# Two transformer blocks on one core: 0/1-matrix products given rounded part and remainder, and halves of squares added by VectorE

## The chip, the cores and the metric

The program runs on one NeuronCore of a Trainium2 chip. The time is device microseconds (us) of one execution of the whole program; lower is better.

## The reference, cut to what matters

`reference(...)` runs two blocks over 256 tokens of 1024 features. The first block mixes tokens with a spatial gate and a bidirectional gated linear attention (four heads, value width 256), whose outputs are normed per head: `o = o * rsqrt(mean(o*o) + eps)`. A convolutional feed-forward follows. The second block prepends 16 tokens (272 in all), runs a gated DeltaNet layer with eight heads of width 128 in chunks, and then feed-forwards and a short-convolution mixer. In the DeltaNet layer three parts matter here:

```
a_mat = I + strict_lower((k_beta @ k.T) * decay)      # one per chunk and head
u = triangular_solve(a_mat, v_beta, lower=True)
...
o = o * rsqrt(mean(o * o, axis=-1) + RMS_EPS) * norm_w   # per token and head
```

## The kernel before, in words

Features lie on the 128 partitions, tokens along the free dimension. Every linear layer is cut in units of eight 128x128 weight blocks. A weight unit `w_raw` is loaded by SyncE, rounded to float32r by ScalarE (`w_hi`, helper line L1689), its remainder `w_lo` is formed by GpSimd (L673), and TensorE multiplies three single-pass float32r products, hi-hi, hi-lo and lo-hi (L763, L785, L788, L948). Small products that need full precision run as plain float32; each of these appears in the trace as two matmul passes with a weight load each. The order of work on each engine is written out by hand. PSUM banks are passed on through counting semaphores: `banks_free` for the weight tiles in banks 0 to 3, and `taken[b]` with the table `TURN` for stages of the second block. `stage_done` counts finished TensorE stages.

**First block, output squares.** ScalarE squares the attention outputs into `osq` (four heads, two halves, 256 tokens). `output_squares` (L1243 to L1251) multiplies each half by a matrix of constants 1/256, two products per head that accumulate, between the linear layers `w_ga` and `w_gb`. ScalarE then takes the root into `orstd` (L1959 to L1963) and only after that counts `banks_free`, for which the first tile of `w_gb` waits. VectorE's part of this stretch is at L2893 to L2903: gate the outputs, form eight remainders of `gu`, add halves of the `w_ga` tiles.

**Second block, 16-row solves.** The blocks of 16 on the diagonals of the triangular matrices are gathered in `diag16` (24 matrices of 16 columns: 16 from bank 4 through a ScalarE copy at L2257, 8 of the short first chunk written by VectorE in `key_products`, L3196). `spread_rows` (L1384 to L1396) copies row k of each block to all 16 partitions of that block, for k = 0 to 14, by a product with the 0/1 matrix `pick16[:, k]` of 128x128; row k has 24 x (15-k) columns, 360 down to 24. These 15 float32 products are spread over six bank turns `sp0` to `sp5`. ScalarE copies each bank to `spread` and VectorE eliminates (`eliminate`, L3211 to L3218, two chained operations for each k). In VectorE's order this stands between the convolution taps (`taps(11, 12, 13)` at L3388). In TensorE's order `blocks_by_lane`, tile 13 of `a_in`, `spread_rows` and tiles 14 to 17 follow each other. The inverses are then flipped by TensorE (`fI1`, `fI2`), copied by ScalarE and VectorE, and their banks 4 to 7 are taken over by the products `kq1` and `kq2` (L1343).

**Second block, norm factors.** `factor` (L3481 to L3490) sums head squares on VectorE and takes a reciprocal. `norm_root` (L2354 to L2359) takes a root on ScalarE into row 5 of `tok`. `factors` (L1522 to L1529) spreads the eight rows over 128 partitions by float32 products with the 0/1 matrix `sel`, with 8 rows as contraction: 8 heads of 134 tokens (`nbA`, `nbB`, `nbC`) and 8 heads of 128 tokens (`nb2A`, `nb2B`). VectorE and ScalarE gate, round and form remainders (L3513 to L3521), and the layer `a_out` (L948) waits for these head by head.

```
ins = mm(dst, pick16[:, k], diag16[:, :, k + 1:], start=True, stop=True)
ins = mm(banks[BANKS[name][0]][:, i * n:(i + 1) * n], sel[:, hh], tok[:, 5, t0_:t1_], start=True, stop=True)
```

Of the kernel before, what the change touches and what calls it, by code (L numbers as in the profile page):

```python
# [17 lines left out]
F32 = mybir.dt.float32  # L18
# [71 lines left out]
def bass_two_blocks(nc, a, out):  # L90
    ctx = ExitStack()
    with ctx:
# [3 lines left out]
        def at(name, shape, offset, dt=F32):  # L96
            return nc.alloc_sbuf_tensor_at(name, shape, dt, offset=offset)
# [164 lines left out]
        pick16 = at("pick16", [P, BLOCK - 1, P], area_a + 17536)  # L262
        spread = [at(f"spread{i}", [P, 512], area_x + 2048 * i if i < 4 else area_a + 25216 + 2048 * (i - 4)) for i in range(6)]
        diag16 = at("diag16", [P, 3 * HN, BLOCK], arena + 41984)
# [438 lines left out]
        def _(pe):  # L703
# [538 lines left out]
            def output_squares():  # L1242

                for b in range(2):
                    pe.wait_ge(banks_free, TILE0["oms"] + b + 1)
                    pe.wait_ge(osq_ready, 4)
                    for hh in (2 * b, 2 * b + 1):
                        for half in range(2):
                            ins = mm(banks[b][:, (hh % 2) * N1:(hh % 2 + 1) * N1], over_dv, osq[:, hh, half],
                                     start=(half == 0), stop=(half == 1))  # L1250
                    ins.then_inc(oms_done, 1)  # L1251

            by_blocks("w_vs", 2, 0)
# [130 lines left out]
            def spread_rows():  # L1384


                pe.wait_ge(spread_ready, 2)
                read_out("kk0")
                read_out("cd")
                for name, ks in SPREAD.items():  # L1390
                    claim(name)
                    for k in ks:
                        o_, n = SPREAD_AT[k][1], BLOCK - 1 - k
                        dst = banks[BANKS[name][0]][:, o_:o_ + 3 * HN * n].rearrange("p (a n) -> p a n", n=n)
                        ins = mm(dst, pick16[:, k], diag16[:, :, k + 1:], start=True, stop=True)
                    ins.then_inc(stage_done, 1)  # L1396

            def y(c, lv):
# [124 lines left out]
            def factors(name, heads, t0_, t1_):  # L1523

                claim(name)
                n = t1_ - t0_
                for i, hh in enumerate(heads):
                    ins = mm(banks[BANKS[name][0]][:, i * n:(i + 1) * n], sel[:, hh], tok[:, 5, t0_:t1_], start=True, stop=True)
                ins.then_inc(stage_done, 1)  # L1529

            def ba(k):
# [147 lines left out]
        def _(act):  # L1679
# [8 lines left out]
            def fn(out_, in_, f, **kw):  # L1688
                return nc.scalar.activation(out_, in_, f, **kw)  # L1689
# [560 lines left out]
            squared(10)  # L2250
            product_out(2, 3)
            tap3(12)
            rounded(12)
            activated(11)
            squared(11)
            act.wait_ge(stage_done, DONE["cd"])
            fn(diag16[:, 0:2 * HN], banks[4][:, 0:2 * P].rearrange("p (a i) -> p a i", i=BLOCK), ACT.Copy).then_inc(taken[4], 1)  # L2257
            tap3(13)
            rounded(13)
            activated(12)  # L2260
# [93 lines left out]
            def norm_root(j, bank, tk):  # L2354

                act.wait_ge(inv_ms, j + 1)
                fn(tok[:, 5, tk], banks[bank][0:HN, 0:tk.stop - tk.start], ACT.Sqrt).then_inc(taken[bank], 1)
                act.wait_ge(taken[bank], TURN[("ho01", "ho2")[j], bank] + 1)
                act.sem_inc(factor_ready, 1)  # L2359

            a_norm = column("a_norm", 0)

# [263 lines left out]
        def _(dve):  # L2626
# [561 lines left out]
            def key_products(c, exp):  # L3188

                cn, B = CHUNKS[c][1], cb[c]  # L3190
                dve.wait_ge(dd_exp, exp)
                for heads, src, free in staged(f"kk{c}", cn, cn):
                    n = src.shape[1]
                    for i in range(n):
                        hh = heads.start + i
                        dst = src[:, i] if c else diag16[0:cn, 2 * HN + hh]  # L3196
                        ins = v.scalar_tensor_tensor(dst, src[:, i], per_token(c, 5, hh), B["dd"][0:cn, hh],
                                                     ALU.mult, ALU.mult)
                    if c == 0:
                        ins.then_inc(free, 1)  # L3200
                        continue
                    ins.then_inc(mt_scaled, 1)

            def identities():

                v.memset(diag16[:, 2 * HN:], 0.0).then_inc(spread_ready, 1)
                dve.wait_ge(taken[7], TURN["inv", 7])
                link(v.tensor_copy(inv16, lanes(eye16[:], 3 * HN)))

            def eliminate(k0, k1_):  # L3210

                for k in range(k0, k1_):
                    n, (name, o_) = BLOCK - 1 - k, SPREAD_AT[k]
                    b = BANKS[name][0]
                    dve.wait_ge(taken[b], TURN[name, b] + 1)
                    row = spread[list(SPREAD).index(name)][:, o_:o_ + 3 * HN * n].rearrange("p (a n) -> p a n", n=n)
# [265 lines left out]
            def factor(j, name, tk):  # L3482

                dve.wait_ge(stage_done, DONE[name])
                total, n = tok[:, 9, tk], tk.stop - tk.start
                for g in range(4):
                    part = banks[BANKS[name][0]][32 * g:32 * g + HN, 0:n]
                    link(v.scalar_tensor_tensor(total, part, 1 / P, total, ALU.mult, ALU.add))
                bank = banks[BANKS[name][0]][0:HN, 0:n]
                v.reciprocal(bank, total).then_inc(inv_ms, 1)  # L3490

            outputs("ov1", 0, 1, 2)
            outputs("ov1", 1, 1, 3)
# [548 lines left out]
```

## Time and profile before

| | |
|---|---|
| three runs | 1243.83, 1244.70, 1246.42 us |
| median | 1244.7 us |
| span of the profiled execution | 1243.2 us |
| TensorE busy, matmuls | 1223.5 us (98%) |
| VectorE, ScalarE, GpSimd busy | 736.0, 722.2, 880.3 us |
| mean granted TensorE clock | 0.993 |

The time of the profiled execution is listed only as its span, from the first to the last instruction; what lies around it isn't listed apart. PE is TensorE's matmuls, PEld its weight loads, DVE VectorE, ACT ScalarE, POOL GpSimd. A row of a timeline gives the start, the duration, the engine, the line and the number of merged instructions; idle time ahead of a row stands in square brackets with what ended it. TensorE's matmuls are pipelined, so the time that each takes from the stream is the distance between starts and not its duration.

### The profile page before, as it was taken

Reading aid. Unit: us, or ns where it says so; the run is one execution under the profiler, and the core shown is the slowest. Engines: PE = TensorE matmul, PEld = TensorE weight load, DVE = VectorE, ACT = ScalarE, POOL = GpSimd, SP = SyncE. Lnnn points to the kernel's source line nnn. Section 1 sums busy time; section 2 is a strip of 40 time slices with the busy share of each in tenths; the row PEclk is TensorE's granted clock in tenths of the full one; section 3 lists DMA queues with packets and bytes.
Section 4 is the critical chain, followed back from the end, with each engine's and each line's share of the span. In section 5 each row is a group of like instructions: output and inputs, shape, how many; then the busy total and the mean of one; then the engine's idle time right before and its main releaser. Section 6 shows DMA issues by size and latency. Waiting matters only on the chain.

```text
span 1243.2 us, 26081 instructions
## 1 busy us (share of the span) xinstructions
PE 1223.5 (98%) x9026; PEld 1127.9 (91%) x9026; DVE 736.0 (59%) x1718; ACT 722.2 (58%) x1325; POOL 880.3 (71%) x387
## 2 busy tenths in 40 slices
PE   9999999999999999999999999999999999999997
PEld 3678899988998888889999999999999999999986
DVE  3989972244587774159884375555634757555633
ACT  3656654565666665479642366666655547666753
POOL 0357857568869888957533248888898868888795
PEclk9999999999999999999998999999999999999999
DMA  9995355446646665645332126555566555656562
GB/s 369 408 366 186 102 187 153 119 149 205 183 142 210 190 186 164 188 146 162 118 98 75 52 88 190 182 183 172 159 187 196 174 166 170 193 180 185 154 200 71
DMA packets 66038, 217.76 MB, mean 175 GB/s; under 512 B 9904, under 2 KB 17328, under 8 KB 62624
## 3 DMA queue, kind: packets, MB, share of 16 engines
q1 hardware_dynamic: 65952, 216.59, 55.0%
q8 instruction: 57, 0.93, 0.3%
q14 instruction: 29, 0.24, 0.1%
HBM read 215.52 MB, written 1.05 MB: 174 GB/s over the span
## 4 chain that ended last, share of the span: by engine, by line
issue 38%; POOL 37%; PE 22%; ACT 1%; POOLq 1%; DVE 1%; ACTq 0%; DVEq 0%
POOL w_lo L673 36%; PE bank L802 10%; PE bank L1135 5%; PE bank L894 3%; PE bank L903 1%; PE bank L898 1%; POOL w_lo L680 1%; POOLq L670 0%; ACT h L1689 0%; ACT w_hi L1689 0%; POOLq L672 0%; PE bank L948 0%; PE bank L724 0%; PE bank L729 0%; PE bank L725 0%
## 5 line engine op out<-in xcount | busy, mean ns | idle before, releaser
L673 POOL TENSOR_TENSOR w_lo<-w_raw,w_hi 128x1024 fp32r<-128x1024 f32 x340 | 812.8, 2404 | 325.1 <-ACT w_hi L1689 323.7
L1689 ACT ACTIVATE w_hi<-w_raw 128x1024 fp32r<-128x1024 f32 (+1 forms) x372 | 378.1, 1020 | 103.0 <-PE bank L903 34.8
L802 PE MATMUL bank<-a_hi,w_hi 128*128 128x264 f32 (+3 forms) x704 | 200.5, 285 | 0.6 <-DVE a_lo L3670 0.6
L802 PE MATMUL bank<-a_hi,w_lo 128*128 128x264 f32 (+3 forms) x704 | 200.2, 284 | 0.0
L802 PE MATMUL bank<-a_lo,w_hi 128*128 128x264 f32 (+3 forms) x704 | 199.9, 284 | 0.0
L802 PEld LDWEIGHTS bank<-a_hi,w_hi 128*128 128x128 f32 x704 | 132.9, 189 | 0.8 <-DVE a_lo L3670 0.8
L802 PEld LDWEIGHTS bank<-a_lo,w_hi 128*128 128x128 f32 x704 | 132.9, 189 | 0.1
L802 PEld LDWEIGHTS bank<-a_hi,w_lo 128*128 128x128 f32 x704 | 132.9, 189 | 0.0
L3745 DVE SCALAR_TENSOR_TENSOR bank<-row_mean,cols,bank 128x260 f32<-128x260 f32 (+3 forms) x112 | 54.6, 488 | 115.8 <-ACT cols L1689 113.0
L763 PE MATMUL bank<-a_parts,w_hi 128*128 128x256 f32 x448 | 81.5, 284 | 0.5 <-DVE a_parts L2952 0.4
L894 PE MATMUL bank<-g_parts,w_hi 128*128 128x512 f32 x308 | 78.9, 396 | 0.0
L680 POOL TENSOR_TENSOR w_lo<-w_raw,w_hi x32 | 58.1, 1844 | 24.0 <-ACT w_hi L1689 23.1
L3042 DVE SCALAR_TENSOR_TENSOR cbuf<-bank,pv,cbuf 128x189 f32<-128x189 f32 (+2 forms) x176 | 65.7, 424 | 14.4 <-ACT cbuf L1689 13.8
L763 PE MATMUL bank<-a_hi,w_hi 128*128 128x272 f32 (+1 forms) x240 | 72.2, 301 | 0.4 <-POOL w_lo L673 0.4
L763 PEld LDWEIGHTS bank<-a_parts,w_hi 128*128 128x128 f32 x448 | 69.8, 192 | 1.2 <-DVE a_parts L2952 0.6
L763 PE MATMUL bank<-a_hi,w_lo 128*128 128x272 f32 (+1 forms) x240 | 70.3, 293 | 0.0
L763 PE MATMUL bank<-a_lo,w_hi 128*128 128x272 f32 (+1 forms) x240 | 70.2, 293 | 0.0
L785 PE MATMUL bank<-a_parts,w_hi 128*128 128x512 f32 x256 | 64.3, 393 | 0.3 <-ACTq L1963 0.3
L894 PEld LDWEIGHTS bank<-g_parts,w_hi 128*128 128x128 f32 x308 | 54.9, 188 | 10.2
L808 PE MATMUL bank<-a_parts,w_hi 128*128 128x512 f32 x256 | 64.1, 392 | 0.0
L931 PE MATMUL bank<-g_parts,w_hi 128*128 128x260 f32 x352 | 63.8, 284 | 0.0
L763 PE MATMUL bank<-a_parts,w_lo 128*128 128x256 f32 x224 | 63.4, 283 | 0.0
(548 smaller groups left out, 2933.1 us busy)
## 6 DMA issues: line engine op xcount, KB each, us to landing
w_raw<-in_s SPq DMA_DIRECT2D x284, 512.0 KB, 3.6
w_raw<-in_down SPq DMA_DIRECT2D x48, 512.0 KB, 3.5
adaw<-in_w_ada SPq DMA_DIRECT2D x16, 1024.0 KB, 9.7
w_raw<-in_down SPq DMA_DIRECT2D x24, 384.0 KB, 3.3
adab<-in_w_ada_first SPq DMA_DIRECT2D x8, 1024.0 KB, 8.7
ctxt<-in_ctx SPq DMA_DIRECT2D x1, 1024.0 KB, 11.3
x<-in_x SPq DMA_DIRECT2D x1, 1024.0 KB, 15.3
out_h<-h SPq DMA_DIRECT2D x4, 256.0 KB, 2.6
```

What stands on the lines that cost most here:

```text
L673: pool.tensor_tensor(w_lo[:, s], w_raw[:, s], w_hi[:, s].bitcast(F32), ALU.subtract) \
L680: pool.tensor_tensor(w_lo[:, :, ds(k, 1)], w_raw[:, :, ds(k, 1)], w_hi[:, :, ds(k, 1)].bitcast(F32), ALU.subtract) \
L763: ins = mm(banks[s][:, first:n], w_[:, s, k], x_[:, k, first:n], start=(m == 0), stop=(m == 3 * KD - 1))
L785: mm(banks[s][:, :].rearrange("p (two n) -> p two n", two=2), w_hi[:, s, k], a_parts[:, :, k, cols], start=(k == 0), stop=False)
L802: ins = mm(banks[bank][:, tk], w_[:, s, k], x_[:, k, tk], start=(m == 0), stop=(m == 3 * KD - 1))
L808: mm(banks[bank][:, :].rearrange("p (two n) -> p two n", two=2), w_hi[:, s, k], a_parts[:, :, k, N1:], start=(k == 0), stop=False)
L894: mm(dst[:, :].rearrange("p (two n) -> p two n", two=2), w_hi[:, s, k], g_parts[:, :, kk, first:n], start=(kk == 0), stop=False)
L931: ins = mm(banks[t][:, first:N2], w_[:, s, k], x_[:, k0 + k, first:N2], start=(m == 0), stop=(m == 3 * KF - 1))
L1135: ins = mm(banks[b][:, :].rearrange("p (u m) -> p u m", u=SLOTS), x_[:, k, tk], w_[:, :, k], start=(k == 0 and i == 0), stop=(k == KD - 1 ...
L1689: return nc.scalar.activation(out_, in_, f, **kw)
L3042: v.scalar_tensor_tensor(dst, frm(banks[banks_of(p)[0]][:, 0:n]), pv[:, ds(pair + w, 1)], dst, ALU.mult, ALU.add).then_inc(conv_seq, 1)
L3745: return v.scalar_tensor_tensor(dst, row_mean[:, N2 - dst.shape[-1]:], by, dst, ALU.mult, ALU.add)
```

## The change

Three edits. `pick16` becomes float32r; the diagonal blocks are stored row-major (`[P, 16, 24]`) as a rounded part `diag_hi` and a remainder `diag_lo`, each row is spread by two accumulating float32r products, and the spread rows lie column-major. The head factors are stored as rounded part in rows 0 to 7 and remainder in rows 32 to 39 of `rows_r`, and each head is spread by one float32r product with contraction 128. The two halves of each head's output squares are added by VectorE, so that one product per head is left.

```diff
-                pe.wait_ge(osq_ready, 4)
+                pe.wait_ge(osq_ready, 5)
 for hh in (2 * b, 2 * b + 1):
-    for half in range(2):
-        ins = mm(banks[b][...], over_dv, osq[:, hh, half], start=(half == 0), stop=(half == 1))
+    ins = mm(banks[b][...], over_dv, osq[:, hh, 0], start=True, stop=True)
 ...
 # VectorE, after the four o_gated products, ahead of the gu remainders
+v.tensor_tensor(osq[:, :, 0], osq[:, :, 0], osq[:, :, 1], ALU.add).then_inc(osq_ready, 1)
 ...
 # spread_rows, TensorE
-pe.wait_ge(spread_ready, 2)
+pe.wait_ge(spread_ready, 3)
-dst = banks[...][:, o_:o_ + 3 * HN * n].rearrange("p (a n) -> p a n", n=n)
-ins = mm(dst, pick16[:, k], diag16[:, :, k + 1:], start=True, stop=True)
+dst = banks[...][:, o_:o_ + 3 * HN * n].rearrange("p (n a) -> p n a", n=n)
+mm(dst, pick16[:, k], diag_hi[:, k + 1:], start=True, stop=False)
+ins = mm(dst, pick16[:, k], diag_lo[:, k + 1:], start=False, stop=True)
 ...
 # ScalarE: ahead of rounded(12) instead of behind squared(11)
+act.wait_ge(stage_done, DONE["cd"])
+fn(diag_hi[:, :, 0:2 * HN].rearrange("p i a -> p a i"), banks[4][:, 0:2 * P]..., ACT.Copy).then_inc(taken[4], 1)
 rounded(12)
 activated(11)
 squared(11)
-act.wait_ge(stage_done, DONE["cd"])
-fn(diag16[:, 0:2 * HN], banks[4][:, 0:2 * P]..., ACT.Copy).then_inc(taken[4], 1)
 ...
 # VectorE
-taps(11, 12, 13)
+dve.wait_ge(taken[5], TURN["kk0", 5] + 1)
+link(v.tensor_copy(diag_hi[:, :, 2 * HN:], diag16[:].rearrange("p a i -> p i a")))
+v.tensor_tensor(diag_lo[:, :, 2 * HN:], diag16[:]..., diag_hi[:, :, 2 * HN:]..., ALU.subtract).then_inc(spread_ready, 1)
+taps(11, 12)
+dve.wait_ge(taken[4], TURN["cd", 4] + 1)
+v.tensor_tensor(diag_lo[:, :, 0:2 * HN], banks[4][:, 0:2 * P]..., diag_hi[:, :, 0:2 * HN]..., ALU.subtract).then_inc(spread_ready, 1)
+taps(13)
 ...
 # eliminate: the spread row is read with a step of 24 elements
-row = spread[...][:, o_:o_ + 3 * HN * n].rearrange("p (a n) -> p a n", n=n)
+row = spread[...][:, o_:o_ + 3 * HN * n].rearrange("p (n a) -> p a n", n=n)
 ...
 # factors, TensorE
-ins = mm(banks[...][:, i * n:(i + 1) * n], sel[:, hh], tok[:, 5, t0_:t1_], start=True, stop=True)
+ins = mm(banks[...][:, i * n:(i + 1) * n], sel_r[:, hh], rows_r[:, 0, t0_:t1_], start=True, stop=True)
 ...
 # norm_root, ScalarE
-fn(tok[:, 5, tk], banks[bank][...], ACT.Sqrt).then_inc(taken[bank], 1)
-act.wait_ge(taken[bank], TURN[("ho01", "ho2")[j], bank] + 1)
-act.sem_inc(factor_ready, 1)
+fn(tok[:, 5, tk], src, ACT.Sqrt)
+fn(rows_r[0:HN, 0, tk], src, ACT.Sqrt).then_inc(taken[bank], 1)
 ...
 # factor, VectorE, behind the reciprocal
+dve.wait_ge(taken[b], TURN[name, b] + 1)
+v.tensor_tensor(rows_r[32:32 + HN, 0, tk], tok[:, 5, tk], rows_r[0:HN, 0, tk]..., ALU.subtract).then_inc(factor_ready, 1)
```

## Rows read from the trace of the kernel before

**Rows 1.** The profile's page: span, and TensorE's busy time.

```profile
span 1243.2 us, 26081 instructions
PE 1223.5 (98%) x9026; PEld 1127.9 (91%) x9026; DVE 736.0 (59%) x1718; ACT 722.2 (58%) x1325; POOL 880.3 (71%) x387
```

**Rows 2.** Busy by stretch: length, PE, PEld, DVE, ACT, POOL, granted clock, DMA, GB/s.

```profile
667.00:674.00 7.00, 7.00 (x52) 6.61 (x51) 2.24 (x5) 0.75 (x2) 1.26 (x1) 0.51 0.26 77
...
721.00:726.00 5.00, 5.00 (x31) 5.00 (x30) 4.37 (x10) 3.17 (x6) 2.02 (x1) 0.66 0.36 102
```

**Rows 3.** Timeline, all engines, around the output squares of the first block.

```profile
251.99 3.62 PE L1249 MATMUL bank<-osq,averages 128*128 128x256 f32 x16
...
253.42 0.38 ACT L1689 ACTIVATE ga<-bank 128x256 f32 x1
...
253.81 1.28 ACT L1689 ACT_TABLE_LOAD   x1
255.10 1.49 ACT L1689 ACTIVATE orstd<-bank,eps 128x512 f32<-128x512 f32 x2
...
255.89 2.12 PE L785 MATMUL bank<-a_parts,w_hi 128*128 128x512 f32 x8 [0.28 <-ACTq L1963]
```

**Rows 4.** Timeline, TensorE, the spread rows and the tile behind them.

```profile
597.47 5.77 PE L1395 MATMUL bank<-diag,pick 128*128 128x360 f32 x30
603.08 0.37 PE L763 MATMUL bank<-a_hi,w_hi 128*128 128x272 f32 x1
```

**Rows 5.** Timeline, TensorE, eight float32r products of 512 and eight of 256 columns.

```profile
249.19 2.00 PE L785 MATMUL bank<-a_parts,w_hi 128*128 128x512 f32 x8
251.04 1.11 PE L788 MATMUL bank<-a_parts,w_lo 128*128 128x256 f32 x8
```

**Rows 6.** Timeline, VectorE, from the taps to the elimination.

```profile
594.47 3.02 DVE L3154 SCALAR_TENSOR_TENSOR qr<-bank,pv,qr 128x269 f32<-128x269 f32 x6
598.01 1.57 DVE L3154 SCALAR_TENSOR_TENSOR qr<-bank,pv,qr 128x269 f32<-128x269 f32 x3 [0.53 <-ACT qr L1689]
600.21 0.53 DVE L3217 TENSOR_TENSOR term<-spread,bank 128x360 f32<-128x360 f32 x1 [0.64 <-ACT spread L1689]
...
610.84 0.28 DVE L3217 TENSOR_TENSOR term<-spread,bank 128x120 f32<-128x120 f32 x1
```

**Rows 7.** Timeline, ScalarE, copies of the first three bank turns.

```profile
599.61 1.53 ACT L1689 ACTIVATE spread<-bank 128x504 f32<-128x504 f32 x3
```

**Rows 8.** Timelines, the flipped inverses: VectorE's copies, and the products behind them.

```profile
621.09 1.28 DVE L3259 COPY tt<-bank 128x512 f32<-128x512 f32 x2
...
621.71 3.84 PE L1343 MATMUL bank<-qr,kr 128*128 128x128 f32 x32 [0.26 <-ACT tt L1689]
```

**Rows 9.** Timelines, TensorE, VectorE and ScalarE around the norm factors.

```profile
708.37 1.60 PE L1528 MATMUL bank<-tok,sel_r 8*128 8x134 f32 x12 [0.78 <-ACT mt L1689]
...
709.90 0.49 PE L1519 MATMUL bank<-qr,s2b 128*128 128x128 f32 x2
...
717.17 0.95 DVE L3490 RECIPROCAL bank<-tok 8x128 f32<-8x128 f32 x1
...
718.15 0.27 ACT L1689 ACTIVATE tok<-bank 8x128 f32<-8x128 f32 x1 [3.29 <-DVE bank L3490]
...
718.58 2.05 PE L1528 MATMUL bank<-tok,sel_r 8*128 8x128 f32 x16
```

**Rows 10.** Timelines, VectorE's last remainders and the eighth block of `a_out`.

```profile
726.48 0.62 DVE L3521 SCALAR_TENSOR_TENSOR a_lo<-bank,pv,a_hi 128x134 fp32r<-128x134 f32 x2 [0.24 <-ACT a_hi L1689]
...
727.68 0.28 PE L948 MATMUL bank<-a_hi,w_hi 128*128 128x262 f32 x1
```

**Rows 11.** Instructions of three VectorE lines: durations in ns, start in us.

```profile
L2670 DVE TENSOR_REDUCE eye<-ident x1: 368/368/368, 3.6 to 3.6; 128x16 f32<-128x128 f32 x1
...
L2675 DVE TENSOR_REDUCE block_of<-ident x1: 275/275/275, 4.2 to 4.2; 128x8 f32<-128x128 f32 x1
...
L3350 DVE TENSOR_TENSOR rows_r<-tok,rows_r x1: 1930/1930/1930, 563.0 to 563.0; 8x272 fp32r<-8x272 f32 x1
```

More of the change, by code:

```diff
@@ L260, in bass_two_blocks @@
         cb[2]["vb"] = at("vb2", [P, HN, P], area_a + 17536 + 8704)
-        pick16 = at("pick16", [P, BLOCK - 1, P], area_a + 17536)
+        pick16 = at("pick16", [P, BLOCK - 1, P], area_a + 17536, F32R)
         spread = [at(f"spread{i}", [P, 512], area_x + 2048 * i if i < 4 else area_a + 25216 + 2048 * (i - 4)) for i in range(6)]
-        diag16 = at("diag16", [P, 3 * HN, BLOCK], arena + 41984)
+        diag16 = at("diag16", [P, HN, BLOCK], arena + 41984)
+        diag_hi = at("diag_hi", [P, BLOCK, 3 * HN], arena + 54272, F32R)
+        diag_lo = at("diag_lo", [P, BLOCK, 3 * HN], arena + 55808, F32R)
         term16 = at("term16", [P, 3 * HN, BLOCK - 1], arena + 43520)
@@ L1245, in output_squares @@
                     pe.wait_ge(banks_free, TILE0["oms"] + b + 1)
-                    pe.wait_ge(osq_ready, 4)
+                    pe.wait_ge(osq_ready, 5)
                     for hh in (2 * b, 2 * b + 1):
-                        for half in range(2):
-                            ins = mm(banks[b][:, (hh % 2) * N1:(hh % 2 + 1) * N1], over_dv, osq[:, hh, half],
-                                     start=(half == 0), stop=(half == 1))
+                        ins = mm(banks[b][:, (hh % 2) * N1:(hh % 2 + 1) * N1], over_dv, osq[:, hh, 0], start=True, stop=True)
                     ins.then_inc(oms_done, 1)
@@ L1393, in spread_rows @@
                         o_, n = SPREAD_AT[k][1], BLOCK - 1 - k
-                        dst = banks[BANKS[name][0]][:, o_:o_ + 3 * HN * n].rearrange("p (a n) -> p a n", n=n)
-                        ins = mm(dst, pick16[:, k], diag16[:, :, k + 1:], start=True, stop=True)
+                        dst = banks[BANKS[name][0]][:, o_:o_ + 3 * HN * n].rearrange("p (n a) -> p n a", n=n)
+                        mm(dst, pick16[:, k], diag_hi[:, k + 1:], start=True, stop=False)
+                        ins = mm(dst, pick16[:, k], diag_lo[:, k + 1:], start=False, stop=True)
                     ins.then_inc(stage_done, 1)
@@ L1527, in factors @@
                 for i, hh in enumerate(heads):
-                    ins = mm(banks[BANKS[name][0]][:, i * n:(i + 1) * n], sel[:, hh], tok[:, 5, t0_:t1_], start=True, stop=True)
+                    ins = mm(banks[BANKS[name][0]][:, i * n:(i + 1) * n], sel_r[:, hh], rows_r[:, 0, t0_:t1_], start=True, stop=True)
                 ins.then_inc(stage_done, 1)
@@ L2252, in _ @@
             tap3(12)
+            act.wait_ge(stage_done, DONE["cd"])
+            fn(diag_hi[:, :, 0:2 * HN].rearrange("p i a -> p a i"), banks[4][:, 0:2 * P].rearrange("p (a i) -> p a i", i=BLOCK), ACT.Copy).then_inc(taken[4], 1)
             rounded(12)
@@ L2255, in _ @@
             squared(11)
-            act.wait_ge(stage_done, DONE["cd"])
-            fn(diag16[:, 0:2 * HN], banks[4][:, 0:2 * P].rearrange("p (a i) -> p a i", i=BLOCK), ACT.Copy).then_inc(taken[4], 1)
             tap3(13)
@@ L2356, in norm_root @@
                 act.wait_ge(inv_ms, j + 1)
-                fn(tok[:, 5, tk], banks[bank][0:HN, 0:tk.stop - tk.start], ACT.Sqrt).then_inc(taken[bank], 1)
-                act.wait_ge(taken[bank], TURN[("ho01", "ho2")[j], bank] + 1)
-                act.sem_inc(factor_ready, 1)
+                src = banks[bank][0:HN, 0:tk.stop - tk.start]
+                fn(tok[:, 5, tk], src, ACT.Sqrt)
+                fn(rows_r[0:HN, 0, tk], src, ACT.Sqrt).then_inc(taken[bank], 1)
             a_norm = column("a_norm", 0)
@@ L3195, in key_products @@
                         hh = heads.start + i
-                        dst = src[:, i] if c else diag16[0:cn, 2 * HN + hh]
+                        dst = src[:, i] if c else diag16[0:cn, hh]
                         ins = v.scalar_tensor_tensor(dst, src[:, i], per_token(c, 5, hh), B["dd"][0:cn, hh],
@@ L3204, in identities @@
             def identities():
-                v.memset(diag16[:, 2 * HN:], 0.0).then_inc(spread_ready, 1)
+                v.memset(diag16[:], 0.0)
                 dve.wait_ge(taken[7], TURN["inv", 7])
@@ L3215, in eliminate @@
                     dve.wait_ge(taken[b], TURN[name, b] + 1)
-                    row = spread[list(SPREAD).index(name)][:, o_:o_ + 3 * HN * n].rearrange("p (a n) -> p a n", n=n)
+                    row = spread[list(SPREAD).index(name)][:, o_:o_ + 3 * HN * n].rearrange("p (n a) -> p a n", n=n)
                     link(v.tensor_tensor(term16[:, :, 0:n], row, inv16[:, :, k:k + 1].broadcast_to([P, 3 * HN, n]), ALU.mult))
@@ L3387, in _ @@
             key_products(0, 3)
-            taps(11, 12, 13)
+            dve.wait_ge(taken[5], TURN["kk0", 5] + 1)
+            link(v.tensor_copy(diag_hi[:, :, 2 * HN:], diag16[:].rearrange("p a i -> p i a")))
+            v.tensor_tensor(diag_lo[:, :, 2 * HN:], diag16[:].rearrange("p a i -> p i a"), diag_hi[:, :, 2 * HN:].bitcast(F32), ALU.subtract).then_inc(spread_ready, 1)
+            taps(11, 12)
+            dve.wait_ge(taken[4], TURN["cd", 4] + 1)
+            v.tensor_tensor(diag_lo[:, :, 0:2 * HN], banks[4][:, 0:2 * P].rearrange("p (a i) -> p i a", i=BLOCK),
+                            diag_hi[:, :, 0:2 * HN].bitcast(F32), ALU.subtract).then_inc(spread_ready, 1)
+            taps(13)
             eliminate(0, 7)
@@ L3490, in factor @@
                 v.reciprocal(bank, total).then_inc(inv_ms, 1)
+                b = BANKS[name][0]
+                dve.wait_ge(taken[b], TURN[name, b] + 1)
+                v.tensor_tensor(rows_r[32:32 + HN, 0, tk], tok[:, 5, tk], rows_r[0:HN, 0, tk].bitcast(F32), ALU.subtract) \
+                    .then_inc(factor_ready, 1)
             outputs("ov1", 0, 1, 2)
```

## The prediction

> **What bounds the kernel now.** I read the page first. TensorE is busy for 98% of a span of 1243.2 us [rows 1], so its stream sets the time, and an edit counts only by what it takes out of that stream or what idle time it puts in. Then I read the clock by stretches. It is at full speed (2.4 GHz) almost everywhere. It falls to half, 1.2 GHz, for about 7 us from 667 on, after a run of small 64-row products, and for about 3.4 us from 721.9 on, after the norm factors [rows 2]. At last I read the three places of the change in the timelines: what TensorE does, and which other engine it meets next. The sums are against the profiled execution, whose own time is listed only as the span; 1243.2 is 1.5 us under the median of 1244.7, and I carry the differences over to the median.
>
> **Output squares.** Now 8 products are 16 passes of 256 columns. Their starts are (3.62 - 0.38) / 15 = 0.216 us apart [rows 3], that is 0.84 ns a column. The edit takes out 8 passes, 1.7 us of TensorE. But who waits next? The first tile of `w_gb` waits for ScalarE's root of the first bank. ScalarE ends the last sigmoid of `w_ga` at 253.80, loads the table for the root for 1.28 us and begins the root at 255.10. TensorE has ended its squares just before and still waits 0.28 us, until 255.89 [rows 3]. None of ScalarE's steps follows from the squares: with two products the first bank is full at 253.0 instead of 253.9, both before 255.10. So TensorE stops 1.7 us earlier and restarts at the same 255.89: the wait grows from 0.3 to 2.0 us and the gain is nothing. VectorE's new add has 1024 columns. By VectorE's slope, (0.53 - 0.28) us over 240 columns [rows 6], it takes some 1.2 us. Behind it stand the eight `gu` remainders and the first half-sum of `w_ga`, for which ScalarE's sigmoid waits; the bank of that tile is wanted only four tiles (11 us) later, so I cost the delay at nothing. **Term: 0.0.**
>
> **Spread rows.** Now the 15 products, 30 passes, run from 597.47 to 603.08, 5.61 us [rows 4]. At 0.84 ns for each of 2 x 2880 columns that is 4.9 us. Take off 0.3 us of a bank wait; what is left, 0.4 us, falls on the narrow passes, which therefore stand at least about 0.10 us apart, against 0.02 us of columns in the narrowest. I read that as the weight load of 128 columns.
>
> After the change there are 30 float32r products of the same widths. Eight products of 512 columns stand (2.00 - 0.39) / 7 = 0.230 us apart, of 256 columns (1.11 - 0.28) / 7 = 0.118 [rows 5]: 0.44 ns a column and 0.006 us. No row shows a float32r product under 256 columns, and ten of the fifteen widths are under it. The cheapest that I can argue is the weight-load floor, 0.105 us; the dearest is what float32 pays for the same columns in its two passes, 1.69 ns each. I take the cheap end, since the rows from 512 to 256 columns lie on one line. Then the widths 360 to 240 give 0.164 + 0.153 + 0.143 + 0.132 + 0.122 + 0.111 and nine others 0.105 each: 1.77 us, twice 3.5 us.
>
> The start moves too. VectorE began `taps(11)` at 594.47 and now first does a copy and a subtraction of 128 elements, 0.3 us each by the 120-element row, and a link: 0.6 us. Taps 11 and 12 take 3.0 us, then comes the new subtraction of 256 elements, about 0.43 us between the rows of 120 and 360 [rows 6]. It ends at 594.47 + 0.6 + 3.0 + 0.43 = 598.5, so TensorE starts at 598.6 instead of 597.47: a new stall of 1.1 us. Behind it ScalarE's copies still begin at 599.61, as ScalarE is busy with tile 13 until then, and end 0.5 us apart [rows 7]. The fourth turn waits for the first copy (600.2), the fifth for the second (600.65), the sixth for the third (601.2); the sixth has ten products, 1.05 us. End 602.25 against 603.08: 0.8 us gained of 2.1. The ScalarE copy that moves ahead of a weight rounding delays that rounding by 1 us; its unit is wanted four tiles, over 9 us, later: nothing.
>
> Does the 0.8 survive? VectorE begins the elimination at 600.21 as before and is busy without a break until its copies of the flipped inverses, from 621.09 to 622.3. TensorE starts the products behind them at 621.71 and needs VectorE's first copy (done 621.73) only for the second four heads, 0.9 us on [rows 8]. So it can come up to 0.9 us earlier. **Term: -0.8.**
>
> **Norm factors.** The first 12 passes take 709.90 - 708.37 = 1.53 us [rows 9]; six float32r products at 0.12 us take 0.7: -0.8. Their start is set by a bank and hides the second root and the new subtraction. Further on the second group's chain has no slack: the reciprocal ends at 718.12, the root at 718.42, and the products start at 718.58 [rows 9]. A second root (0.2) and a subtraction with its hop (0.35) come in, partly against a slack of 0.1: +0.45 for these products. They shrink from 1.98 us to about 0.95. TensorE thus gains about 1.4 us until `a_in`'s last tile. Then `a_out` wants remainders head by head. VectorE's last ends at 727.10, TensorE needs it at 727.68 [rows 10]; that chain moves by -0.8 + 0.2 (the second root ahead of ScalarE's rounding) = -0.6, to 726.5. TensorE arrives no later than 726.4 even if the clock falls again, so VectorE's chain ends last: 727.68 - 726.5. **Term: -1.2.**
>
> **Sum:** 0.0 - 0.8 - 1.2 = -2.0 us: span 1241.2, median 1242.7.
>
> **A rule against the change.** The elimination's 15 multiplications read 2880 elements of spread rows one after another; each element now lies 96 bytes from the last. Two early reductions over the same 128 elements show what a step may cost: 368 ns with 64 bytes between elements, 275 ns in order [rows 11], 0.73 ns an element. For 2880 that would be 2.1 us; if the 93 ns are the cost of shorter groups it is nothing, which I take as likelier. The Trainium skill, SBUF — State Buffer, on cachelines, says that each access that crosses to another 16-byte line pays a penalty. By that rule the multiplications are slower, and the two reductions agree with it in sign. A second row matters for the new subtractions whose inputs both lie in SBUF: L3350 took 1.93 us for 272 columns [rows 11], where 0.43 would be expected. If the one at 595 meets the same, TensorE's stall grows by up to 1.5 us; that end I keep for the range. The same page, on the shared port pair, says that a VectorE instruction with two SBUF inputs is blocked for the length of a GpSimd instruction that reads SBUF.
>
> **Rivals.**
> - *Narrow float32r products at float32's price.* For: no product under 256 columns is in the trace. Against: nothing but the line from 512 to 256. Ten widths at 1.69 ns a column (floor 0.105) give 2.3 us, five wide ones 0.7, twice 3.0 = 6.1 us from 598.6 on: TensorE goes on at 604.7, +1.6. The factors gain 0.2 before and lose 0.35 in the chain: +0.2. Time 1246.5, slower than before; it decides from a price of about 1.2 ns a column on, where the stall is no longer paid back.
> - *Stepped reads cost 0.73 ns an element.* VectorE's chain grows 2.1 us, of which 0.9 is slack at the flipped inverses: +1.2 instead of -0.8. Time 1244.7.
> - *The squares do gain*, if ScalarE's table load follows them after all: -1.7 more, 1241.0. The load begins right at the end of the sigmoid [rows 3], which speaks against it.
> - *The clock.* Idle or thinner work may bring one more stretch at half clock, or take one away: 3.4 us at half cost 1.7 us [rows 2], 1244.4 or 1241.0 from the forecast.
>
> **How the numbers follow.** Forecast 0.42; narrow price 0.30; stepped reads 0.18; squares 0.03; clock or other 0.07. The range: 1240.9 to 1247.0 takes in a clock stretch less on one side, the narrow price and part of a blocked subtraction on the other. A measurement here tells some 0.2%, 2.5 us, from no change. My forecast of -2.0 lies just inside; with the scatter of runs (1243.8 to 1246.4) I give it a 0.4 chance to pass: 0.17, and 0.08 from the squares and the clock. The narrow price passes +2.5 in a third: 0.10, others 0.05. Faster 0.25, same 0.60, slower 0.15.
>
> **What would show it.** The squares: L785's idle ahead of `w_gb` at 2.0 us, orstd's start against the sigmoid's end unchanged. The spread: TensorE's idle ahead of it 1.1 us, and the distance of starts of the 96-column products, 0.105 or 0.16. The elimination: L3217 at 360 columns 0.53 or 0.8 us. The factors: starts 0.12 us apart, or 0.22. The prediction is wrong if `w_gb` starts earlier after the sigmoid, if the narrow starts are at the float32 price, or if TensorE waits for VectorE at the flipped inverses.

## The result and the profile after

The changed kernel takes 1247.88 us (median of 10 runs, 1245.13 to 1250.29) against 1244.8 us before (10 runs, 1243.83 to 1246.42): ratio 1.0023, interval 1.0015 to 1.0032. That is slower by 2.9 us, where 2.0 us faster was forecast, and outside the range of 1240.9 to 1247.0. The profiled execution took 1248.83 us, span 1247.0. From the profile's page of the changed kernel:

```profile
span 1247.0 us, 26039 instructions
PE 1222.0 (98%) x9002; PEld 1126.4 (90%) x9002; DVE 741.0 (59%) x1724; ACT 722.8 (58%) x1327; POOL 881.4 (71%) x387
```

VectorE is busy for 741.0 us instead of 736.0; TensorE's share of 98% is the old one [rows 1]. Next the table of TensorE's waits in the changed kernel, dearest first (what it waited for, us in total, times, longest):

```profile
PE bank L1316 <- ACT ksq L1690: 2.6, 1, 2.6
PE bank L787 <- ACTq L1964: 2.0, 1, 2.0
...
PE bank L1395 <- DVE diag_lo L3395: 1.1, 1, 1.1
...
PE bank L950 <- DVE a_lo L3534: 0.9, 2, 0.6
```

The waits ahead of `w_gb` (L787) and of the spread products (L1395) were forecast, at 2.0 and 1.1 us. The first, 2.6 us for ScalarE's `ksq`, stands nowhere in the prediction. Two places in TensorE's timeline of the changed kernel, the squares [rows 3] and the spread rows [rows 4]:

```profile
251.62 1.89 PE L1250 MATMUL bank<-osq,averages 128*128 128x256 f32 x8
255.52 3.29 PE L787 MATMUL bank<-a_parts,w_hi 128*128 128x512 f32 x8 [2.01 <-ACTq L1964]
...
599.11 0.43 PE L1395 MATMUL bank<-diag_hi,pick 128*128 128x360 f32 x1 [1.14 <-DVE diag_lo L3395]
...
602.05 0.26 PE L1395 MATMUL bank<-diag_hi,pick 128*128 128x96 f32 x1
602.15 0.28 PE L1396 MATMUL bank<-diag_lo,pick 128*128 128x96 f32 x1
...
602.92 0.37 PE L765 MATMUL bank<-a_hi,w_hi 128*128 128x272 f32 x1
```

From squares to `w_gb` are 3.90 us, as before. The narrow float32r products start 0.10 us apart: the cheap price, so the rival with 0.30 of the chance is out at once. From the end of the tile ahead (599.11 - 1.14 = 597.97) to the next tile are 4.95 us, where before there were 603.08 - 597.47 = 5.61: 0.66 gained, 0.8 forecast. The stage itself does what was said. Now VectorE's timeline behind it [rows 6], and TensorE's at the next meeting, the key norms and the products behind the flipped inverses [rows 8]:

```profile
595.39 0.38 DVE L3392 TENSOR_TENSOR diag_lo<-diag,diag_hi 128x128 fp32r<-128x128 f32 x1
...
598.64 0.41 DVE L3395 TENSOR_TENSOR diag_lo<-bank,diag_hi 128x256 fp32r<-128x256 f32 x1
598.97 1.56 DVE L3156 SCALAR_TENSOR_TENSOR qr<-bank,pv,qr 128x269 f32<-128x269 f32 x3
600.79 0.95 DVE L3219 TENSOR_TENSOR term<-spread,bank 128x360 f32<-128x360 f32 x1 [0.27 <-ACT spread L1690]
601.78 0.54 DVE L3220 TENSOR_TENSOR bank<-bank,term 128x360 f32<-128x360 f32 x1
...
615.20 1.57 DVE L3156 SCALAR_TENSOR_TENSOR qr<-bank,pv,qr 128x269 f32<-128x269 f32 x3
```

```profile
617.75 1.86 PE L1316 MATMUL bank<-ksq,pick 128*8 128x272 f32 x16 [2.57 <-ACT ksq L1690]
...
625.64 3.84 PE L1343 MATMUL bank<-qr,kr 128*128 128x128 f32 x32 [0.27 <-ACT tt L1690]
```

The multiplication of 360 columns takes 0.95 us instead of 0.53; the sum behind it, whose operands are all in PSUM or in order, still 0.54. The fifteen multiplications take 8.52 us together, where before they took 5.34: 3.2 us more, and the elimination also begins 0.58 later. Inside the elimination stands the last tile of taps of `qr` (615.20 here, 611.48 before). ScalarE squares it, and TensorE's key norms wait for that square. Before, the square was there at 614.3, 1.1 us ahead of TensorE at 615.38; now it is 2.6 us late.

Last, the granted clock. Stretches of the changed kernel (start and end in us, length, TensorE busy, granted clock, DMA share, GB/s):

```profile
255.00:260.00 5.00, 4.48 (x17) 0.66 0.53 175
617.00:622.00 5.00, 4.25 (x29) 0.66 0.35 105
641.00:646.00 5.00, 4.76 (x66) 0.66 0.38 111
672.00:680.00 8.00, 8.00 (x64) 0.57 0.23 68
```

Half clock falls in this execution behind the idle 2.0 us ahead of `w_gb`, behind the idle 2.6 us ahead of the key norms, and behind the small 32-row products at 641; the stretch at 672 was there before, and the one behind the norm factors [rows 2] is gone. Counted together that is two stretches of 3.4 us more than before, some 1.7 us each.

### The profile page after: what moved, and what is told of

It is laid out like the page before. It is cut to its first block, busy times and chain, and to the rows that moved or that the text cites. A ratio compares the mean times of both kernels' runs of the same rounds, so it can differ in the third digit from the quotient of the medians.

```text
span 1247.0 us, 26039 instructions
## 1 busy us (share of the span) xinstructions
PE 1222.0 (98%) x9002; PEld 1126.4 (90%) x9002; DVE 741.0 (59%) x1724; ACT 722.8 (58%) x1327; POOL 881.4 (71%) x387
## 4 chain that ended last, share of the span: by engine, by line
issue 38%; POOL 37%; PE 22%; ACT 1%; POOLq 1%; DVE 1%; ACTq 0%; DVEq 0%
POOL w_lo L675 37%; PE bank L804 10%; PE bank L1137 5%; PE bank L896 3%; PE bank L905 1%; PE bank L900 1%; POOL w_lo L682 1%; POOLq L672 0%; ACT h L1690 0%; ACT w_hi L1690 0%; POOLq L674 0%; PE bank L726 0%; PE bank L950 0%; PE bank L731 0%; PE bank L727 0%
## 5 line engine op out<-in xcount | busy, mean ns | idle before, releaser
L787 PE MATMUL bank<-a_parts,w_hi 128*128 128x512 f32 x256 | 65.5, 398 | 2.0 <-ACTq L1964 2.0
```

The lines of the kernel that those rows point to most:

```text
L787: mm(banks[s][:, :].rearrange("p (two n) -> p two n", two=2), w_hi[:, s, k], a_parts[:, :, k, cols], start=(k == 0), stop=False)
```

## The experiments

All comparisons are with the kernel before, run on the same chip beside them: 1244.54 us (31 runs) for the first four, 1244.4 us (33 runs) for the next four, 1244.3 us (17 runs) for the last three.

### The three edits one at a time, and the order alone

**e_sq** is the kernel before with only this:

```diff
-                    pe.wait_ge(osq_ready, 4)
+                    pe.wait_ge(osq_ready, 5)
-                        for half in range(2):
-                            ins = mm(..., osq[:, hh, half], start=(half == 0), stop=(half == 1))
+                        ins = mm(..., over_dv, osq[:, hh, 0], start=True, stop=True)
+            v.tensor_tensor(osq[:, :, 0], osq[:, :, 0], osq[:, :, 1], ALU.add).then_inc(osq_ready, 1)
```

> Before with the squares' edit alone. Theory A (the idle time costs clock): TensorE stops 1.7 us earlier, w_gb still starts where it did, idle ahead of it 2.0 us instead of 0.3, and the clock falls to half for some 3.4 us right behind it, which costs 1.7 us: 1246.4 us. Theory B (the edit is neutral, the half-clock stretch seen there belongs to something else): 2.0 us of idle, clock full, 1244.7 us.

Measured: 1245.29 us, ratio 1.0006 (0.9997 to 1.0015). Timeline of TensorE and the clock of two stretches in its profiled execution:

```profile
251.99 1.89 PE L1248 MATMUL bank<-osq,averages 128*128 128x256 f32 x8
255.89 2.12 PE L785 MATMUL bank<-a_parts,w_hi 128*128 128x512 f32 x8 [2.01 <-ACTq L1961]
...
255.00:260.00 5.00, 4.11 (x22) 1.00 0.58 186
637.00:642.00 5.00, 5.00 (x55) 0.66 0.38 108
```

`w_gb` starts at 255.89, to the hundredth where it started before [rows 3]: the idle time took the whole saving. The same 2.0 us of idle time left the clock at full here and at half in the changed kernel; instead half clock came at 638, where the profiled execution of before has none, and the stretch behind the norm factors [rows 2] stayed away, so the two executions spent the same time at half clock. So theory A's 1.7 us are not paid each time. Over the runs the mean granted clock is 0.9937 against 0.9945 before; 0.0008 of 1243 us is 1.0 us, and the means of the spans differ by 0.9 (1243.8 against 1242.9). The ratio's interval holds 1, so a cost of the squares' edit is not shown, only that it brings nothing.

**e_fac** is the kernel before with only this:

```diff
-  ins = mm(banks[...][:, i * n:(i + 1) * n], sel[:, hh], tok[:, 5, t0_:t1_], start=True, stop=True)
+  ins = mm(banks[...][:, i * n:(i + 1) * n], sel_r[:, hh], rows_r[:, 0, t0_:t1_], start=True, stop=True)
+  fn(rows_r[0:HN, 0, tk], src, ACT.Sqrt).then_inc(taken[bank], 1)
+  v.tensor_tensor(rows_r[32:32 + HN, 0, tk], tok[:, 5, tk], rows_r[0:HN, 0, tk]..., ALU.subtract).then_inc(factor_ready, 1)
```

> Before with the factors' edit alone. Theory A: the products start 0.118 us apart or less and TensorE is 1.2 to 1.6 us earlier at a_in's last tile; a_out then waits for VectorE's remainders, about -1.0 us in all, 1243.7 us, and 1242.0 if the half-clock stretch behind the factors goes as it did in the changed kernel. Theory B (the gain in the changed kernel was the clock's alone, the new root and subtraction eat the rest): 1244.7 us.

Measured: 1242.48 us, ratio 0.9981 (0.9971 to 0.999): the edit gains 2.1 us. TensorE's timeline:

```profile
704.75 0.86 PE L1528 MATMUL bank<-rows_r,sel_r 128*128 128x134 f32 x6 [0.78 <-ACT mt L1689]
...
714.43 1.11 PE L1528 MATMUL bank<-rows_r,sel_r 128*128 128x128 f32 x8 [0.29 <-DVE rows_r L3493]
...
721.14 0.39 PE L948 MATMUL bank<-a_hi,w_hi 128*128 128x262 f32 x1 [0.29 <-DVE a_lo L3525]
```

Eight products last 1.11 us, so their starts are (1.11 - 0.28) / 7 = 0.119 apart. Between the first factor product and the eighth block of `a_out` lie 17.65 us here (704.75 to 722.40) and 18.63 in e_sq (709.21 to 727.84), both without half clock in between: 1.0 us is the edit's own. The other 1.1 us of the medians may be the clock's, which these runs do not separate: the mean granted clock rises from 0.9945 to 0.9964, and this execution has no half-clock stretch before 1230 us.

**e_spr** is the kernel before with only the spread edit: the split of the diagonal blocks, fifteen products in two parts, rows laid `(n a)`, and the multiplication reading them with steps.

```diff
+  dst = ...rearrange("p (n a) -> p n a", n=n)
+  mm(dst, pick16[:, k], diag_hi[:, k + 1:], start=True, stop=False)
+  ins = mm(dst, pick16[:, k], diag_lo[:, k + 1:], start=False, stop=True)
-  row = spread[...][:, o_:o_ + 3 * HN * n].rearrange("p (a n) -> p a n", n=n)
+  row = spread[...][:, o_:o_ + 3 * HN * n].rearrange("p (n a) -> p a n", n=n)
```

> Before with the spread edit alone. Theory A (VectorE's stepped reads of the spread rows): L3217's 360-column multiplication takes 0.95 us instead of 0.53, the elimination ends 3.2 to 3.8 us later, TensorE waits about 2.6 us for the squares of tile 15 ahead of the key norms, with a half-clock stretch behind it: 1248 us with one such stretch, 1246.4 with none, 1249.8 with two. Theory B (the cost is the stall of 1.1 us ahead of the products and the two-part products, VectorE's delay being slack): 1244.7 us or below.

Measured: 1247.59 us, ratio 1.0026 (1.0017 to 1.0035). TensorE's timeline at the key norms and behind them:

```profile
619.61 1.10 PE L1318 MATMUL bank<-ksq,pick 128*8 128x272 f32 x16 [2.56 <-ACT ksq L1692]
...
625.28 1.53 PE L1370 MATMUL bank<-ident,uu 128*128 128x128 f32 x12 [0.92 <-DVE tok L3412]
```

The multiplication of 360 columns takes 0.96 us and the wait ahead of the key norms 2.56, as in the changed kernel. The half-clock stretch that theory A put behind this wait did not come: the granted clock from 619 to 624 is 1.00. This profiled execution, the slowest of its eleven runs (1252.43 us), has its half clock at 543, 642, 673 and 717. The three parts alone make +0.06, -0.19 and +0.26 per cent, together +0.13; the whole has +0.23. Each has an interval of about 0.09 to either side, so the parts add up as far as these runs tell.

**e_step** keeps float32 products, without split, subtraction or stall, and changes only the order:

```diff
-  dst = ...rearrange("p (a n) -> p a n", n=n)
+  dst = ...rearrange("p (n a) -> p a n", n=n)
-  row = spread[...]....rearrange("p (a n) -> p a n", n=n)
+  row = spread[...]....rearrange("p (n a) -> p a n", n=n)
```

> Before with the spread rows' order alone: float32 products as before that write each row's 24 groups side by side, and multiplications that read them with 96 bytes between elements; no split, no new subtraction. Theory A (the stepped reads are the cause): multiplications of 360 columns 0.95 us, elimination 3.8 us longer, TensorE waits 2 to 3 us ahead of the key norms, 1247 to 1248.5 us. Theory B (the stepped reads cost little and the two-part form or its stall is the cause): 0.53 to 0.6 us and 1244.7 us.

Measured: 1248.01 us, ratio 1.0023 (1.0013 to 1.0033). The order alone costs as much as the spread edit as a whole. VectorE's and TensorE's timelines:

```profile
599.30 0.95 DVE L3217 TENSOR_TENSOR term<-spread,bank 128x360 f32<-128x360 f32 x1 [0.63 <-ACT spread L1689]
```

```profile
596.61 5.71 PE L1395 MATMUL bank<-diag,pick 128*128 128x360 f32 x30
602.16 0.37 PE L763 MATMUL bank<-a_hi,w_hi 128*128 128x272 f32 x1
...
616.26 1.10 PE L1316 MATMUL bank<-ksq,pick 128*8 128x272 f32 x16 [1.81 <-ACT ksq L1689]
621.93 1.53 PE L1368 MATMUL bank<-ident,uu 128*128 128x128 f32 x12 [0.90 <-DVE tok L3402]
```

The same 0.95 us with no float32r in sight, and TensorE waits twice, 1.8 us for the square of tile 15 and 0.9 for VectorE's row of `tok` behind the copies into blocks. From the first spread product to the products behind the flipped inverses are 26.69 us (596.61 to 623.30) against 24.24 before (597.47 to 621.71), 2.45 more, with the clock full throughout. TensorE's own writes with steps of 96 bytes into PSUM cost it nothing: from the first spread product to the next tile are 5.55 us (596.61 to 602.16), against 5.61 before [rows 4].

### What a step costs

**e_steps** puts twenty multiplications of 360 columns behind the elimination of the kernel before; nothing of it but their durations is used.

```diff
+  for s_ in (1, 2, 3, 4, 6, 8, 12, 24, 60, 120):
+      for src_ in (spread[0], banks[7]):
+          v.tensor_tensor(term as [P, s_, 360 // s_], src_[:, 0:360].rearrange("p (n s) -> p s n", s=s_), one column, ALU.mult)
```

> Before with twenty multiplications of 360 columns put behind the elimination (their results are overwritten unused): ten read one operand from SBUF, ten from PSUM, with 1, 2, 3, 4, 6, 8, 12, 24, 60 and 120 elements between neighbours. Only their durations are wanted. Theory A (a step costs in SBUF, by the line that it crosses to, and not in PSUM): SBUF 0.53 us in order, rising to a plateau of about 0.95 us once neighbours lie 16 bytes or more apart; PSUM 0.53 to 0.58 us at every step. Theory B (the price is one of short runs of elements): SBUF and PSUM alike grow with the number of runs, dearest at 60 and 120.

VectorE's timeline, in the order of the loop. `term<-spread` reads SBUF and `term<-bank` reads PSUM, each pair with the next step. Left out are the second pair (0.53 us both), the SBUF row of 6 elements (0.81) and the PSUM rows of 3 elements (0.54) and of 4, 6, 8, 12 and 60, all 0.53:

```profile
614.50 0.53 DVE L3396 TENSOR_TENSOR term<-spread,bank 128x360 f32<-128x360 f32 x1
615.07 0.53 DVE L3396 TENSOR_TENSOR term<-bank,spread 128x360 f32<-128x360 f32 x1
...
616.76 0.65 DVE L3396 TENSOR_TENSOR term<-spread,bank 128x360 f32<-128x360 f32 x1
...
618.02 0.81 DVE L3396 TENSOR_TENSOR term<-spread,bank 128x360 f32<-128x360 f32 x1
...
620.84 0.80 DVE L3396 TENSOR_TENSOR term<-spread,bank 128x360 f32<-128x360 f32 x1
...
622.25 0.78 DVE L3396 TENSOR_TENSOR term<-spread,bank 128x360 f32<-128x360 f32 x1
...
623.63 0.95 DVE L3396 TENSOR_TENSOR term<-spread,bank 128x360 f32<-128x360 f32 x1
624.62 0.53 DVE L3396 TENSOR_TENSOR term<-bank,spread 128x360 f32<-128x360 f32 x1
625.19 0.81 DVE L3396 TENSOR_TENSOR term<-spread,bank 128x360 f32<-128x360 f32 x1
...
626.60 0.57 DVE L3396 TENSOR_TENSOR term<-spread,bank 128x360 f32<-128x360 f32 x1
627.20 0.53 DVE L3396 TENSOR_TENSOR term<-bank,spread 128x360 f32<-128x360 f32 x1
```

SBUF in order, and with one element between, 0.53; with neighbours 12 bytes apart 0.65; 16 to 48 bytes 0.78 to 0.81; 96 bytes 0.95; 240 bytes 0.81; 480 bytes, where only three elements follow one another, 0.57. PSUM is 0.53 or 0.54 at every step. So SBUF pays for steps and PSUM does not, as theory A says, and theory B, by which both would pay, is out. Theory A's plateau isn't there: 96 bytes is dearer than 16 to 48, and 480 bytes costs almost nothing. Here the run of elements between two jumps back gets shorter as the step grows, so this kernel alone doesn't tell the two apart. Its one execution took 1257.7 us, with the twenty multiplications in it. The Trainium skill, SBUF — State Buffer, on cachelines, puts a penalty on each access that crosses to another 16-byte line. These rows agree for SBUF from 16 bytes on; for the three-element runs, each element on a line of its own, they don't.

### The stepped reads taken away

**e_inv** is the changed kernel with the block inverses and the terms laid out like the spread rows, so that the multiplications read in order. The steps that remain are in PSUM reads.

```diff
-        inv16 = banks[7][...].rearrange("p (a i) -> p a i", i=BLOCK)
+        inv16 = banks[7][...].rearrange("p (i a) -> p a i", i=BLOCK)
-        term16 = at("term16", [P, 3 * HN, BLOCK - 1], arena + 43520)
+        term16 = at("term16", [P, BLOCK - 1, 3 * HN], arena + 43520)
-                    row = ...rearrange("p (n a) -> p a n", n=n)
+                    row = ...rearrange("p (n a) -> p n a", n=n)
+                    inv = inv16.rearrange("p a i -> p i a")
```

> The changed kernel with the elimination's own tiles turned too: the block inverses in PSUM and the terms are laid out with their 24 groups side by side, so that every operand of the multiplications and sums is read in order; the only stepped reads left are those of PSUM by the two copies into blocks. Theory A (the stepped SBUF reads are the cause of the slower time): multiplication of 360 columns 0.53 to 0.58 us, no wait of 2.6 us ahead of the key norms, the copies into blocks 1.17 us each as before, spread edit worth -0.6, with the squares' +0.7 and the factors' -2.0 as measured: 1242.6 us. Theory B (a step costs the same wherever it is read, so the cost moves to the copies into blocks): those copies 1.8 us each or more, 1245 us or above.

Measured: 1243.31 us, ratio 0.9988 (0.9977 to 0.9998), where the changed kernel has 1.0023, each against the kernel before run beside it: 4.6 us between the two medians. VectorE, then TensorE at the key norms:

```profile
601.08 0.53 DVE L3220 TENSOR_TENSOR term<-spread,bank 128x360 f32<-128x360 f32 x1 [0.27 <-ACT spread L1690]
...
616.07 2.33 DVE L3227 TENSOR_TENSOR uu<-bank,block_of 128x1024 f32<-128x1024 f32 x2
```

```profile
615.39 1.10 PE L1316 MATMUL bank<-ksq,pick 128*8 128x272 f32 x16
```

0.53 again, the fifteen multiplications 5.27 us together, no wait ahead of the key norms, and the two copies into blocks, which now read PSUM with steps, take 2.33 us as before. The cost did not move, it is gone. (The squares' 2.0 us of idle time are still in this kernel, and here half clock stands behind them again, 0.66 from 255 to 260.)

### The squares' saving brought into the open

**e_evac** is the kernel before with the squares' edit, and VectorE empties the two banks, so that `w_gb` no longer waits for ScalarE's table load and root. ScalarE's part of the edit isn't shown: it takes the root from VectorE's copy and no longer counts the banks as free.

```diff
+  for b in range(2):
+      dve.wait_ge(oms_done, b + 1)
+      v.tensor_copy(orstd[:, 2 * b:2 * b + 2], banks[b]...).then_inc(ostd_ready, 1)
+  dve.wait_ge(ostd_ready, 2)
+  dve.wait_ge(banks_free, TILE0["oms"] + 4)
+  dve.sem_inc(banks_free, 4)
   for b in range(2):
       ins = v.reciprocal(orstd[:, hs], orstd[:, hs])
+      add_gate_half("w_gb", b)
```

> Before with the squares' edit, and VectorE copies the two banks of mean squares to SBUF and frees them, so that ScalarE's table load and root are no longer between the squares and w_gb; the reciprocal's two halves are followed each by a half-sum of w_gb. Theory A (the 1.7 us of products saved are real, only the root's place hid them): w_gb starts 3.9 - 1.7 = 2.2 us after the squares start, idle about 0.3 us, nothing new behind it: 1244.5 - 1.6 = 1242.9 us. Theory B (VectorE's reciprocal of 6.6 us, which still follows the root, holds the banks and the roundings of w_gb): TensorE waits 1 us or more inside w_gb, 1244 to 1244.7 us.

Measured: 1244.14 us, ratio 0.9997 (0.9988 to 1.0006). The timelines of TensorE and VectorE:

```profile
254.76 2.11 PE L785 MATMUL bank<-a_parts,w_hi 128*128 128x512 f32 x8 [0.87 <-DVEq L2909]
```

```profile
253.93 0.69 DVE L2906 COPY orstd<-bank 128x512 f32<-128x512 f32 x1 [0.17 <-PE bank L1248]
```

`w_gb` starts 2.76 us after the squares instead of 3.90: 1.1 us are there in the trace, and TensorE does not wait inside `w_gb`, so theory B's mechanism is out. The remaining 0.9 us of idle time is the second copy, behind which both banks were freed. The median is where theory B had it all the same, 1.2 us above theory A's: 1.1 us is too small to be told from nothing here.

**e_nospr** is e_evac with the factors' edit, spread rows as before. **e_best** is the changed kernel with e_inv's and e_evac's edits.

> Before with the squares' edit and its early copies, and the factors' edit; spread rows as before. Theory A (the parts add up): -1.6 and -2.0: 1240.9 us. Theory B (the gains are shares of one slack, or of the clock): 1242.5 us.

> The changed kernel with the turned elimination and the early copies of the mean squares: all three edits with what hid or spoiled them taken away. Theory A: -1.6 squares, -0.6 spread rows, -2.0 factors: 1240.3 us. Theory B (the spread edit gains nothing even with reads in order, since TensorE's stall of 1.1 us and the later elimination eat it): no better than the same kernel without the spread edit, 1240.9 us or above.

Measured: 1241.82 us, ratio 0.9986 (0.9977 to 0.9995), and 1241.60 us, 0.9975 (0.9964 to 0.9985). Both were forecast about 1 us too low. Their intervals overlap. In e_best the spread products start at 596.59 behind their stall of 1.1 us, so the tile ahead ended at 595.45, and the products behind the flipped inverses start at 619.00, 23.55 us later. In e_nospr the same way, where no stall stands ahead, takes 24.16 us (596.58 to 620.74). So the spread edit, read in order, takes 0.6 us out of TensorE's stream, as in the changed kernel's own stage. That it counts in the total is not shown.

### Two stalls left

**e_early** is e_inv with the subtraction of 256 columns ahead of the tile of taps 12:

```diff
-            taps(11, 12)
+            taps(11)
             ... diag_lo[:, :, 0:2 * HN] ...
-            taps(13)
+            taps(12, 13)
```

> The changed kernel with the turned elimination, and the subtraction of 256 columns one tile of taps earlier. Theory A (the stall of 1.1 us is covered by the waits for ScalarE's copies that follow in the same stage): products start 1 us earlier, wait inside the stage instead, the next tile starts 0.2 us earlier at most: 1243.2 us against 1243.3 without it. Theory B (the stall is lost time): 1242.2 us.

Measured: 1243.02 us, ratio 0.9986 (0.9976 to 0.9997), against e_inv's 0.9988: no difference that can be told. TensorE's timeline shows why:

```profile
597.94 0.27 PE L1396 MATMUL bank<-diag_lo,pick 128*128 128x192 f32 x1
599.49 0.40 PE L1395 MATMUL bank<-diag_hi,pick 128*128 128x288 f32 x1 [1.28 <-ACT spread L1690]
```

The wait of 1.15 us ahead of the products became one of 1.28 us inside them, for ScalarE's copy of the first turn. From the last product of the tile ahead to the products behind the flipped inverses are 23.85 us in e_inv (597.96 to 621.81) and the same in e_early (596.34 to 620.19). ScalarE's copies set this stage's pace, and theory A holds.

**e_best2** is e_best with e_early's edit, and bank 0 freed right behind its own copy:

```diff
+                dve.wait_ge(ostd_ready, b + 1)
+                dve.wait_ge(banks_free, TILE0["oms"] + 4 + b)
+                dve.sem_inc(banks_free, 3 if b else 1)
```

> The version with all three edits repaired, with the earlier subtraction too, and with bank 0 of the mean squares freed right behind its copy instead of behind both. Theory A: w_gb starts 2.2 us after the squares instead of 2.76: -0.5, and -0.1 from the subtraction: 1241.0 us. Theory B (what is left between these versions is the clock's scatter): no difference from 1241.6 us.

Measured: 1241.06 us (1239.37 to 1241.68, 7 runs), ratio 0.9971 (0.9959 to 0.9984): 0.29% faster than before, the best of all. TensorE's timeline:

```profile
252.91 1.89 PE L1250 MATMUL bank<-osq,averages 128*128 128x256 f32 x8
254.81 2.14 PE L787 MATMUL bank<-a_parts,w_hi 128*128 128x512 f32 x8
```

`w_gb` follows the squares with no idle time at all, 1.90 us after their start instead of 3.90: 2.0 us of TensorE's stream. Against e_best the medians differ by 0.5 us, as theory A has it, but within the intervals.

## Why the prediction was wrong

**Output squares, right.** "The wait grows from 0.3 to 2.0 us and the gain is nothing": 2.01 us, and `w_gb` at the same time in e_sq. The clock rival named idle time as a risk in general, but put it at no place. A half-clock stretch stands right behind these 2.0 us in the profiles of the changed kernel and of e_inv, and none in e_sq's.

**Spread products, right.** Narrow products 0.10 us apart (0.105 taken), stall 1.14 us (1.1), gain of the stage 0.66 us (0.8). VectorE's small instructions took what was said of them: 0.38 us for 128 elements, 0.41 for 256; the blocked subtraction that was kept for the range did not come.

**Stepped reads, wrong, and this is the step that failed.** The text had the mechanism as a rival, with two rows for it [rows 11], and chose "if the 93 ns are the cost of shorter groups it is nothing, which I take as likelier", at a chance of 0.18. Three things were off.
- The choice. e_step has the whole loss with nothing but the order changed, e_inv has it removed. In the two reductions the step and the shorter groups came together, so they could not decide. e_steps does: 0.95 us with 96 bytes between elements in runs of fifteen, 0.57 in the shortest runs, those of three. So it is not the shortness of the groups that costs.
- The size. 0.73 ns an element was taken from a step of 64 bytes over short groups of eight. Fifteen multiplications of 2880 elements together became 3.2 us longer, 1.10 ns an element, so the rival's 2.1 us were too few as well.
- The place. The rival looked for the delay at the flipped inverses, with 0.9 us of slack. But two tiles of taps stand inside the elimination, and TensorE meets the later of them first, through ScalarE's square of it, ahead of the key norms. The slack there was 1.1 us of VectorE's 3.8. Behind it the copies into blocks and the row of `tok` were late as well, 0.9 us in e_step. The rival's 1.2 us for TensorE was 2.45 in that run with the clock at full.

**Norm factors, right.** 1.2 us forecast; 1.0 us in the timelines that no half-clock stretch disturbs, and 2.1 in the medians of e_fac. The forecast was counted against an execution with half clock in this place: there the way from the first factor product to the eighth block of `a_out` is 19.31 us (708.37 to 727.68), and was forecast at 18.1, where e_fac has 17.65. TensorE does wait for VectorE's remainders at `a_out`, as was said (0.9 us in two waits).

**The clock, priced but not placed.** "One more stretch at half clock" at 1.7 us had, with everything else, a chance of 0.07. The profiled execution has two more than before. Over the ten runs the mean granted clock is 0.9926 against 0.9945 for the kernel before in the 31 runs beside the first experiments. 0.0019 of 1246 us is 2.4 us. That count is rough and can't be added to the others: in the profiled executions the last 4 to 7 us, in which TensorE has no product left, stand at half clock too, which costs nothing but enters the mean. So a part of the 2.9 us may be lost through the clock, and how much stays open: in e_step the same count gives 0.9 us of 3.5, with 2.45 in the timelines.

**The sum.** Stage by stage, where the clock was full: squares 0.0; spread edit +2.6 (in e_spr from the end of the tile ahead, 599.81, to the products behind the flipped inverses, 626.64, against 24.24 us before); factors -1.0. That is +1.6 where -2.0 was forecast, and 3.4 of the difference are the spread edit's. The 1.3 us up to the measured 2.9 are within what the mean clock allows for, but no run shows their cause.

## What to carry to other kernels

When an edit turns a layout so that TensorE writes or reads in order, follow the tile to every engine that reads it next: a VectorE multiplication took half again to nearly double the time when its float32 operand in SBUF had neighbours 16 to 240 bytes apart, and no more for the same steps in PSUM, so put the steps there. Slack is to be looked up at the first meeting behind the delayed chain, and other work woven into the chain meets first. A saving ahead of a wait that does not follow from it only lengthens the wait, until the wait's own cause (here a root that held a bank) is moved.

## What the runs showed of the hardware

- VectorE's price of a step in SBUF is not one number: per 360 elements 0.12 us more at 12 bytes, 0.25 to 0.28 at 16 to 48, 0.42 at 96, 0.28 at 240, and 0.04 where runs are three long. In the changed kernel's elimination the step is 96 bytes throughout and only the runs get shorter: against before an element costs 0.9 to 1.4 ns more in runs of five to fifteen, 0.6 in runs of four, and nothing in runs of three or less.
- TensorE's float32 products took no longer when they wrote PSUM with 96 bytes between elements (5.55 us for thirty passes and their bank waits, 5.61 in order).
- Float32r products of 24 to 96 columns with a stationary matrix of 128 start 0.10 to 0.11 us apart whatever their width.
- Half clock came and went between executions of the same work: behind the same 2.0 us of idle time TensorE's granted clock was 0.66 over 5 us in one kernel and 1.00 in another, and one execution of e_fac ran up to 1230 us with none at all.
